# Conditioning of a hybrid attention and DeltaNet block: w_ada tiles as the stationary operand, loaded in column groups

## What is computed

```python
mod = c @ w_ada + b_ada
shift, scale, gate = jnp.split(mod, 3, axis=-1)
h = rmsnorm(x, pre_norm_gain) * (1.0 + scale[:, None, :]) + shift[:, None, :]
proj = h @ w_in
# ... sparse attention branch, gated DeltaNet branch, merge, output projection
return x + gate[:, None, :] * rmsnorm(out, post_norm_gain)
```

## Time and profile before

| | |
|---|---|
| median of three runs | 899.78 us (899.57 to 900.02) |
| profiled execution, its own time | 899.64 us |
| span in the profile | 897.8 us |
| TensorE matmul, busy | 832.9 us, 93% of the span |
| VectorE, busy | 473.0 us, 53% |
| GpSimd, busy | 392.6 us, 44% |
| ScalarE, busy | 326.7 us, 36% |
| mean granted clock of TensorE | 0.983 of full speed |

### The profile page before, as it was taken

How to read it: one execution, slowest core, us unless ns; L and a number is a source line. 1 busy time by engine, 2 the same in 40 slices (tenths; PEclk the granted TensorE clock), 3 DMA queues, 4 the chain that set the end, 5 groups by cost and what they waited for, 6 DMA issues and landing times.

```text
span 897.8 us, 11319 instructions
## 1 busy us (share of the span) xinstructions
PE 832.9 (93%) x4226; PEld 672.3 (75%) x4226; DVE 473.0 (53%) x907; ACT 326.7 (36%) x678; POOL 392.6 (44%) x262
## 2 busy tenths in 40 slices
PE   1978688999999989999999999999999999999996
PEld 0546565688888778888888777777777788878996
DVE  3455889826668777665666544445434433232104
ACT  2424432444352434425434344443334322212211
POOL 1123554355264434644535544354543543543542
PEclk9989889999999999999999999999999999999998
DMA  7933530533232332323221222232222245452502
GB/s 273 334 88 124 171 92 8 120 103 110 63 104 61 106 81 61 93 61 106 83 70 48 71 70 71 71 92 72 71 71 71 74 142 160 141 171 86 194 19 94
DMA packets 147345, 92.10 MB, mean 103 GB/s; under 512 B 17746, under 2 KB 140883, under 8 KB 146011
## 3 DMA queue, kind: packets, MB, share of 16 engines
q1 hardware_dynamic: 147290, 91.38, 34.9%
HBM read 84.52 MB, written 6.85 MB: 102 GB/s over the span
## 4 chain that ended last, share of the span: by engine, by line
PE 71%; DVE 18%; ACT 4%; issue 3%; DMA 2%; POOL 1%; SPq 0%; POOLq 0%; ACTq 0%; DVEq 0%
PE ps L588 15%; PE ps L590 15%; PE ps L589 15%; PE ps L629 3%; DVE yq L1552 2%; PE ps L859 2%; PE ps L907 2%; PE ps L906 2%; PE ps L905 2%; PE ps L846 2%; DVE binv L1611 2%; ACT prob L1144 2%; DVE kraw L1552 1%; DMA pos_i<-in_positions 1%; DVE prob L1721 1%
## 5 line engine op out<-in xcount | busy, mean ns | idle before, releaser
L1216 POOL TENSOR_TENSOR w_lo<-raw,w_hi 128x1024 fp32r<-128x1024 f32 (+1 forms) x109 | 263.5, 2423 | 351.5 <-ACT w_hi L926 351.4
L588 PE MATMUL ps<-h_hi,w_hi 128*128 128x512 f32 (+1 forms) x680 | 291.0, 428 | 6.0 <-ACT h_hi L948 6.0
L590 PE MATMUL ps<-h_hi,w_lo 128*128 128x512 f32 (+1 forms) x680 | 269.1, 396 | 0.0
L589 PE MATMUL ps<-h_lo,w_hi 128*128 128x512 f32 (+1 forms) x680 | 267.7, 394 | 0.0
L588 PEld LDWEIGHTS ps<-h_hi,w_hi 128*128 128x128 f32 (+1 forms) x680 | 129.8, 191 | 32.5 <-ACT h_hi L948 6.8
L590 PEld LDWEIGHTS ps<-h_hi,w_lo 128*128 128x128 f32 (+1 forms) x680 | 128.8, 189 | 29.8 <-issue 0.5
L589 PEld LDWEIGHTS ps<-h_lo,w_hi 128*128 128x128 f32 (+1 forms) x680 | 129.7, 191 | 26.1 <-issue 3.6
L926 ACT ACTIVATE w_hi<-raw 128x1024 fp32r<-128x1024 f32 (+1 forms) x109 | 113.3, 1050 | 18.2 <-PE ps L907 17.1
L1085 ACT ACTIVATE o_tok<-ps 128x128 f32<-128x128 f32 x32 | 8.9, 278 | 107.4 <-PE ps L811 107.2
L629 PE MATMUL ps<-w_ada_sb,cb 128*128 128x512 f32 x64 | 30.2, 633 | 11.5 <-DVE rp L1376 11.5
L906 PE MATMUL ps<-w_lo,y_hi 128*128 128x256 f32 x128 | 36.2, 283 | 0.0
(11 more groups left out here) (274 smaller groups left out, 1445.8 us busy)
## 6 DMA issues: line engine op xcount, KB each, us to landing
raw<-in_w_in SPq DMA_DIRECT2D x84, 512.0 KB, 3.8
w_ada_sb<-in_w_ada SPq DMA_DIRECT2D x8, 1024.0 KB, 19.5
raw<-in_w_b_out SPq DMA_DIRECT2D x8, 512.0 KB, 3.8
raw<-in_w_a_out SPq DMA_DIRECT2D x8, 512.0 KB, 4.1
ada<-in_w_ada SPq DMA_DIRECT2D x8, 512.0 KB, 4.8
raw<-in_w_o SPq DMA_DIRECT2D x8, 512.0 KB, 4.0
inverse_tiles<-zero SPq DMA_DIRECT2D x2, 1032.0 KB, 5.0
x_sb<-in_x SPq DMA_DIRECT2D x1, 2048.0 KB, 10.0
```

The lines of the kernel that those rows point to most:

```text
L588: pe.matmul(out_ap, w_hi[:, slot, k, 0:m], rhs_hi(k), start=(k == 0), stop=False)
L589: pe.matmul(out_ap, w_hi[:, slot, k, 0:m], rhs_lo(k), start=False, stop=False)
L590: mm = pe.matmul(out_ap, w_lo[:, slot, k, 0:m], rhs_hi(k), start=False, stop=(k == KT - 1))
L1216: pool.tensor_tensor(w_lo[:, slot, :, 0:n], raw[:, slot, :, 0:n], w_hi[:, slot, :, 0:n].bitcast(F32), ALU.subtract).then_inc(lo_made, 1)
```

## The change

w_ada is loaded as four groups of 512 columns instead of eight groups of 128 rows (the same bytes, in rows of 2 KB instead of 8 KB). The first group goes ahead of x, the second and third behind it, and the fourth behind the weights of unit 1. The positions and the two small vectors now go ahead of x too. The product takes each 128x128 tile of w_ada as the stationary operand and one column of c as the moving one, so that the result comes out by channel, one column of PSUM for each of 16 blocks, and VectorE adds b_ada straight out of PSUM. `cb` and the sixteen extractions are gone. Groups 0 to 2 come ahead of the transposes, group 3 behind them. ScalarE rounds the weights of units 2 and 3 within its loop over `h_hi`, and no longer ahead of it.

```diff
-        sp.dma_start(x_sb[:], x.rearrange("(i p) d -> p i d", p=P)).then_inc(s_x, 16)
         sp.dma_start(pos_i[:], positions.to_broadcast([P, S])).then_inc(s_pos, 16)
...
-        for k in range(KT):
-            sp.dma_start(w_ada_sb[:, k, :], w_ada[k * P:(k + 1) * P, 0:2 * D]).then_inc(s_ada[k], 16)
+
+        def conditioning(g):
+
+            sp.dma_start(w_ada_sb[:, :, g * S:(g + 1) * S],
+                         w_ada.rearrange("(k p) n -> p k n", p=P)[:, :, g * S:(g + 1) * S]).then_inc(s_ada[g], 16)
+
+        conditioning(0)
+        sp.dma_start(x_sb[:], x.rearrange("(i p) d -> p i d", p=P)).then_inc(s_x, 16)
+        conditioning(1)
+        conditioning(2)
...
-        for q in range(1, RING):
+        load(1)
+        conditioning(3)
+        for q in range(2, RING):
             load(q)
...
-        EARLY = 4
...
-        def condition(ks):
-            for k in ks:
-                pe.wait_ge(s_ada[k], 16)
-                for n in range(4):
-                    mm = pe.matmul(bank(2 + n), cb[:, k, :], w_ada_sb[:, k, n * S:(n + 1) * S], start=(k == 0),
-                                   stop=(k == KT - 1))
+        def condition(groups):
+            for g in groups:
+                pe.wait_ge(s_ada[g], 16)
+                for b in range(4 * g, 4 * g + 4):
+                    for k in range(KT):
+                        mm = pe.matmul(ps[:, 3, b:b + 1], w_ada_sb[:, k, blk(b)], pcol[:, 0, R_C + k:R_C + k + 1],
+                                       start=(k == 0), stop=(k == KT - 1))
             return mm
 
-        pe.wait_ge(*pro_dve.at("cb"))
         pe.wait_ge(*pro_dve.at("pcol2"))
-        condition(range(EARLY))
+        condition(range(3))
...
-        condition(range(EARLY, KT)).then_inc(*pro_pe.inc("mod"))
+        condition(range(3, 4)).then_inc(*pro_pe.inc("mod"))
...
         split(0, N_SMALL)
-        for q in range(1, RING):
-            split(q)
+        split(1)
         for k in range(KT):
             act.wait_ge(*pro_dve.at(f"h{k}"))
             act.activation(h_hi[:, k, :], xT[:, k, :], ACT.Copy).then_inc(*pro_act.inc(f"hi{k}"))
+            if k % 4 == 3:
+                split(2 + k // 4)
...
-        dve.tensor_copy(cb[:], pcol[:, 0, R_C:R_C + KT].unsqueeze(2).to_broadcast([P, KT, P])).then_inc(*pro_dve.inc("cb"))
...
-        for b in range(16):
-            dve.tensor_tensor_reduce(scratch16[:, b, :], ps[:, 2 + b // 4, blk(b % 4)], ident, 1.0, 0.0, ALU.mult, ALU.add,
-                                     small_cols[:, 8 + b:9 + b]).then_inc(*pro_dve.inc(f"m{b}"))
-        dve.wait_ge(*pro_dve.at("m15"))
-        dve.tensor_tensor(small_cols[:, 8:24], small_cols[:, 8:24], pcol[:, 0, R_BADA:R_BADA + 16], ALU.add).then_inc(
+        dve.tensor_tensor(small_cols[:, 8:24], ps[:, 3, 0:16], pcol[:, 0, R_BADA:R_BADA + 16], ALU.add).then_inc(
             *pro_dve.inc("mb"))
```

More of the change, by code:

```diff
@@ L254, in program @@
     x_sb = place("x_sb", [P, NT, D], at=base + KT * 2 * D * 4)
-    scratch16 = place("scratch16", [P, 16, P], at=base + KT * 2 * D * 4)
     xT = place("xT", [P, KT, S], at=base + KT * 2 * D * 4 + NT * D * 4)
-    cb = place("cb", [P, KT, P], at=base + KT * 2 * D * 4 + NT * D * 4 + KT * S * 4)
     rp = place("rp", [P, 4, 2 * S], at=where["w_lo"])
@@ L327, in program @@
         "residual_loaded", "output_stored"))
-    s_ada = [sem(f"w_ada_loaded{k}") for k in range(KT)]
+    s_ada = [sem(f"w_ada_loaded{g}") for g in range(4)]
     s_raw = [sem(f"weights_loaded{s}") for s in range(RING)]
@@ L342, in program @@
                     + [f"hi{k}" for k in range(KT)])
-    pro_dve = steps("pro_dve", ["pcol", "pcol2", "cb", "hgain", "posf", "angA", "angI", "turns", "whole", "r1", "r2", "r3", "rc",
+    pro_dve = steps("pro_dve", ["pcol", "pcol2", "hgain", "posf", "angA", "angI", "turns", "whole", "r1", "r2", "r3", "rc",
                                 "wrap", "rc2", "clamp", "clampc"]
                     + [f"xn{i}" for i in range(NT)] + [f"x{k}" for k in range(0, KT, 2)]
-                    + [f"m{b}" for b in range(16)] + ["mb", "scg", "h0"]
+                    + ["mb", "scg", "h0"]
                     + [f"{a}{k - (a == 'lo')}" for k in range(1, KT) for a in ("h", "lo")] + [f"lo{KT - 1}"])
```

## The result

| | before | changed |
|---|---|---|
| median of the runs | 899.90 us (899.57 to 900.57) | 914.44 us (913.74 to 915.39) |
| ratio | | 1.0165, 95% interval 1.0153 to 1.0177 |
| profiled execution, its own time | 899.64 us | 914.12 us |
| span | 897.8 us | 912.3 us |
| first product of unit 0 | 59.65 us | 74.95 us |

The changed kernel is 14.5 us slower. The prologue carries all of it: the first product of unit 0 starts 15.3 us later, the time from there until ScalarE takes unit 0's result is 1.2 us shorter (12.20 against 13.36), and the remaining 825 us agree within 0.4 us.

The account below looks back on a forecast made before the run. TensorE was taken to bound the start of unit 0's first product: 16.2 + 41.3 + 7.0 + 13.8 + 0.3 + 2.45 gave 81.0 us against 59.65, so 899.64 + 21.4 = 921.0 us; range 889 to 925.

Parts of the forecast that it names:

- the rival that it was set against: Conditioning on TensorE: the clock rises on weight loads, first product at 54.2 us, kernel faster at 891.2 us; chance 0.28.
- the likeliest case's own range: Whole kernel, with TensorE's clock staying low on the conditioning loads: 914 to 925 us around 921.0; chance 0.64.
- Count and bound: Conditioning product: 128 calls give 256 weight loads, 64 a group; the loads are the bound and the matmul hides behind them.
- Pitch at the low clock: Conditioning on TensorE: one weight load every 0.215 us at the low clock (0.208 to 0.223), 13.8 us a group.
- Which clock: Conditioning on TensorE: the clock starts low and doesn't rise on loads with one moving column; two to one.
- Arrival of group 0: Prologue transfers: the first column group of w_ada is in at 16.2 us, bounds 15 to 18.
- Rivals 2 and 3: Conditioning: loads cost the same at both clocks, 898 us, 0.05; or 2 KB rows at 312 GB/s, 893 to 896, 0.03.
- Transposes: TensorE between groups 2 and 3: 32 transposes at the low clock, 7.0 us; 5 us less if they raise the clock.
- Last steps: From the end of group 3 to unit 0's first product: 0.3 us drain plus 2.45 us of steps.
- After it: Behind unit 0's first product: its first products run at the low clock in both kernels; later rounds 2 us either way.
- Loads: Prologue transfers: 395 GB/s for 2 KB rows, 5.3 us a group, 3.5 us for three transfers, group 3 in at 40.7.
- Moved splits: ScalarE's splits of units 2 and 3, moved into the h_hi loop: 1 us at most if uncovered.

Follow-up runs that it names:

- wide64: The changed kernel with 64 equal columns of c moving in each conditioning product instead of one; 913.44 us, ratio 1.0151.
- wide128: The changed kernel with 128 equal columns of c moving in each conditioning product instead of one; 894.56 us, ratio to before 0.9945.
- wide32: The changed kernel with 32 equal columns of c moving in each conditioning product instead of one; 914.10 us, ratio 1.0165.
- warm_start: The changed kernel with seven products of 512 columns, result unread, on TensorE in the idle time ahead of group 0; 914.44 us, ratio 1.0171.
- x_early: The changed kernel with the transposes of x ahead of group 2 instead of behind it; 915.72 us, ratio 1.0186.
- one_k: The changed kernel with the product for only the first of eight row tiles of w_ada, 16 calls instead of 128, all transfers kept; 888.08 us, ratio 0.9869.
- dve_group: wide128 with group 2 summed over the row tiles by VectorE and its partitions added by four TensorE products; 892.73 us, ratio 0.9919.

## Why the prediction was right, and by how much it was off

The forecast was 921.0, the measured median 914.44. The direction, the mechanism and the rival that it was set against came out as written. Measured against its own step, the shift was put at 21.4 us and is 14.5; 914.44 lies at the edge of the likeliest case's own range (914 to 925). It lies inside it by luck: a term that was 6.7 us too large, against 5 us allowed, was in part made good by group 0's data, 1.1 us late. And the full range, 889 to 925, took in a gain as well as a loss, so that the number alone says little; what carries the forecast is that the loads, their pace and the low clock in groups 0 to 2 came as written. Point by point:

- **Count and bound.** 256 records, the load as the bound, the matmul hidden: right. The earlier trace rows was the right row, and wide64 shows its 0.111 again, wide128 0.112 to 0.114.
- **Pitch at the low clock.** Taken 0.215 between 0.208 and 0.223, measured 0.214. Three groups: 41.3 forecast, 41.09 measured.
- **Which clock.** Two to one for low, and it was low. The argument, that loads are no work for the clock, was only argued then. wide32 and wide128 show it: same loads, and the number of moving columns alone decides.
- **Arrival of group 0.** 16.2 forecast, 17.29 measured: 1.1 us. Why it came later was not looked into.
- **Rivals 2 and 3.** Loads that cost the same at both clocks: not so by warm_start. Rows of 2 KB at 312 GB/s: not so, 385 to 390 GB/s while groups 1 and 2 come in.
- **Transposes.** Here is the step that failed. I took 7.0 us at the low clock and kept "5 us less" as a bound, in case they bring the clock up. They do. They took 5.14 (1.9 less) and group 3 behind them 8.96 in place of 13.8 (4.8 less), 6.7 us together: more than the bound. The rows of before had leaned that way: the clock did not fall during the 3.5 us of transposes, and I set that aside as proving little. The Trainium skill (TensorE: Matmul & The Clock Gate, Part 4), which I cited for keeping the low clock, says that transposes don't count as work for it. This case differs: 11 records stand in the 2 us from 58 and 21 in the 2 us from 62, all within or beside the transposes' 5.14 us, and x_early shows it a second time (5.66 us).
- **Last steps.** 2.75 us for drain and the steps to the first product; measured 74.95 - 72.48 = 2.47. The steps took their 2.45. The 0.3 us for the drain, for which I had shown no row, did not come on top.
- **Sum.** 81.0 + 1.1 - 0.2 - 1.9 - 4.8 - 0.3 = 74.9, and the first product is at 74.95.
- **After it.** Unit 0 at the low clock was taken as equal in both. It ran low for 3.7 us instead of 6, and took 1.2 us less. The rounds took 0.4 us more. Together that is a gain of 0.8 us, within the 2 allowed.
- **Loads.** Data of group 3 at 40.7 forecast; 44.0 in one_k. The arrivals of groups 1 and 2 (27.6 and, in dve_group, 32.9) keep the 5.3 us apart, so 395 GB/s for 2 KB rows holds. If group 3 took 5.3 us as well, the three transfers between groups 2 and 3 took 5.8 us (44.0 - 32.9 - 5.3) and not 3.5. It changed nothing here, but it would be the bound of a faster prologue.
- **Moved splits.** Costed at 1 us at most. In the changed kernel TensorE did not wait for them. With the short conditioning of wide128 they gain 2.4 us, since they move GpSimd's work away from VectorE's first steps of h; that contention was in no term.

## What to carry to other kernels

A product with one moving column isn't cheap on TensorE. It costs its weight load, here 0.11 us for 128 columns of plain float32 and two loads to a call, and the long run of such products here was done at the low clock, at twice that. If the loads are the bound, let as many columns stream as the load covers, even useless equal ones; here 128 in place of 1 turned a loss of 14.5 us into a gain of 5. And when a form seems to save work, ask which row shows it in a long run, since the one row that I had (eight in a row between dense products) showed the full clock.

## What the runs showed of the hardware that was not expected

- **Raising and holding.** With 64 columns the clock stayed low for 41 us, and then stayed high through all of group 3 after the transposes had raised it. 32 columns did not hold it.
- **The fall comes late.** Behind the last transpose the full clock lasted nearly 5 us in the changed kernel and 5.3 us in x_early; in warm_start it was gone 2.3 us behind the last dense product.
- **VectorE and GpSimd.** One of VectorE's steps beside a subtraction of GpSimd took about four times as long. It is so in the changed kernel too (2.75 us at 78.53, GpSimd from 78.06 on). wide128, VectorE and GpSimd:

```profile
58.87 2.75 DVE L1427 TENSOR_TENSOR h_lo<-xT,h_hi 128x512 fp32r<-128x512 f32 x1
```

```profile
58.40 2.67 POOL L1225 TENSOR_TENSOR w_lo<-raw,w_hi 128x1024 fp32r<-128x1024 f32 x1 [7.28 <-ACT w_hi L934]
```

0.69 us is its time alone. It ends 0.55 us behind GpSimd's, at 61.62 against 61.07. In wide128 and in the changed kernel TensorE was busy with earlier tiles; in dve_group, with unit 0 at the full clock, TensorE waited 0.81 us for it. Which of the two engines' operands collide was not tried.
